# A hybrid RWKV-7 / gated-DeltaNet block: the gate pass's banks are emptied right behind two small steps on ScalarE, and three weight splits move back

## The reference, cut to what matters

```python
xn = rmsnorm(x, norm_mix_pre)
p = (xn @ w_in)                                   # 256 x (3 x 2048 + LoRA + 3 x 2048 + z + gates)
# RWKV-7 half, 32 heads x 64
p_rwkv = p_rwkv + (token_shift(p_rwkv) - p_rwkv) * rwkv_mix
kk = l2norm(k * rwkv_k_k);  k = k * (1 + (a - 1) * rwkv_k_a)
y = rwkv7_recurrence(r, decay, k, v, -kk, kk * a)  # then GroupNorm, bonus, gate
# gated DeltaNet half, 16 heads x 128, chunks of 64 frames
qkv = silu(causal_depthwise_conv(p_qkv, gdn_conv_w))
q, k = l2norm(q) * 128 ** -0.5, l2norm(k)
o = gated_delta_rule_chunked(q, k, v, g, beta)
y_b = rmsnorm(o, gdn_norm_w) * silu(z)
mixed = sigmoid(gate_a) * y_a + sigmoid(gate_b) * y_b
x = x + rmsnorm(mixed @ w_out, norm_mix_post)
x = x + rmsnorm((silu(rmsnorm(x) @ w_gate) * (rmsnorm(x) @ w_up)) @ w_down)
```

## Time and profile before

| | |
|---|---|
| time, median of 3 | 2225.74 us (2225.69 to 2225.81) |
| the profiled execution | 2224.51 us, of which the span of the core's instructions is 2222.8 |
| mean granted TensorE clock | 0.98 |
| busy: PE, PEld, DVE, ACT, POOL | 94%, 81%, 64%, 49%, 7% |
| one unit of the loop, q24 to q24 | 77.95 to 79.59 us |

### The profile page before, as it was taken

One profiled execution on the slowest core, in us unless ns is written; L12 is line 12 of the kernel. 1 busy time (PEld: TensorE's weight loads), 2 busy tenths in 40 slices (PEclk: granted clock), 3 DMA queues, 4 the chain that ended last, 5 costly groups with the idle time before them and its releaser, 6 DMA issues. The chain is left out here.

```text
span 2222.8 us, 49299 instructions
## 1 busy us (share of the span) xinstructions
PE 2092.7 (94%) x20515; PEld 1808.3 (81%) x20515; DVE 1420.4 (64%) x2816; ACT 1089.3 (49%) x2051; POOL 160.3 (7%) x277
## 2 busy tenths in 40 slices
PE   5999999999999999999999999499999999999995
PEld 5888888888888888888888889478888888778884
DVE  5568777777877877787787775544544445444444
ACT  4545554655555565555555545434444444344443
POOL 3001011011011101101110110000000000000000
PEclk9999999999999999999999999799999999999998
DMA  7654444545444455444544435175555555545542
GB/s 203 172 142 125 119 122 122 145 120 129 128 126 124 118 131 135 122 124 119 144 119 120 116 111 162 43 246 187 188 189 189 189 189 189 178 161 186 185 186 86
DMA packets 386637, 327.27 MB, mean 147 GB/s; under 512 B 11697, under 2 KB 334225, under 8 KB 379793
## 3 DMA queue, kind: packets, MB, share of 16 engines
q1 hardware_dynamic: 372384, 318.53, 48.8%
q10 hardware_dynamic: 14064, 6.04, 1.1%
HBM read 322.44 MB, written 2.10 MB: 146 GB/s over the span
## 5 line engine op out<-in xcount | busy, mean ns | idle before, releaser
L247 PE MATMUL ps<-hi_all,xh 128*128 128x384 f32 (+1 forms) x1568 | 564.0, 360 | 31.7 <-ACT pu L273 28.9
L1736 DVE TENSOR_TENSOR lo_all<-stage,hi_all 128x1024 fp32r<-128x1024 f32 x264 | 323.3, 1225 | 385.3 <-ACT hi_all L1731 385.3
L249 PE MATMUL ps<-hi_all,xl 128*128 128x384 f32 (+1 forms) x1568 | 531.8, 339 | 0.0
L248 PE MATMUL ps<-lo_all,xh 128*128 128x384 f32 (+1 forms) x1568 | 530.7, 338 | 0.0
L1731 ACT ACTIVATE hi_all<-stage 128x1024 fp32r<-128x1024 f32 x264 | 279.9, 1061 | 433.7 <-PE ps L1749 427.3
L242 DVE TENSOR_TENSOR lo_all<-stage,hi_all 128x768 fp32r<-128x768 f32 (+1 forms) x400 | 377.9, 965 | 120.5 <-ACT hi_all L237 119.7
L237 ACT ACTIVATE hi_all<-stage 128x768 fp32r<-128x768 f32 (+1 forms) x400 | 327.7, 833 | 217.6 <-PE ps L249 210.9
L247 PEld LDWEIGHTS ps<-hi_all,xh 128*128 128x128 f32 x1568 | 295.8, 189 | 67.6 <-ACT pu L273 36.2
L248 PEld LDWEIGHTS ps<-lo_all,xh 128*128 128x128 f32 x1568 | 296.8, 189 | 0.9
L249 PEld LDWEIGHTS ps<-hi_all,xl 128*128 128x128 f32 x1568 | 296.4, 189 | 0.9
L1745 PE MATMUL ps<-hi_all,xh 128*128 128x512 f32 x704 | 276.8, 393 | 10.0 <-DVE lo_all L1736 10.0
(11 more groups left out here) (277 smaller groups left out, 2655.3 us busy)
## 6 DMA issues: line engine op xcount, KB each, us to landing
stage<-in_w_in SPq DMA_DIRECT2D x288, 512.0 KB, 5.7
stage<-in_ffn_w_gate SPq DMA_DIRECT2D x44, 1024.0 KB, 5.2
stage<-in_ffn_w_up SPq DMA_DIRECT2D x44, 1024.0 KB, 5.2
stage<-in_ffn_w_down SPq DMA_DIRECT2D x22, 2048.0 KB, 7.6
stage<-in_w_out SPq DMA_DIRECT2D x16, 344.0 KB, 4.3
stage<-in_w_out SPq DMA_DIRECT2D x8, 516.0 KB, 4.6
stage<-in_w_in SPq DMA_DIRECT2D x8, 448.0 KB, 6.9
stage<-in_w_out SPq DMA_DIRECT2D x8, 336.0 KB, 4.6
```

The costliest lines, as they stand in the source:

```text
L247: nc.tensor.matmul(o, xh[:, kc, xs], high, start=kc == 0, stop=False)
L248: nc.tensor.matmul(o, xh[:, kc, xs], low, start=False, stop=False)
L249: return nc.tensor.matmul(o, xl[:, kc, xs], high, start=False, stop=kc == KC - 1)
L1736: nc.vector.tensor_tensor(wlo[s.par], src, whi[s.par].bitcast(F32), ALU.subtract).then_inc(s.lo, 1)
```

## The change

`chunk_act` gets a callback that it runs right behind its copy of r. The ACT list of a unit now has the squares, `r2`, `take_out(2)`, the two `stw` scalings (wa2, wb2), step (2, 2) with the two copies of u2, and then both weight splits (quanta 26 and 27) at once; one of them stood ahead of `r2` before, the other behind `take_out`. In unit 0 there is no r2, and `take_out` stands right behind the squares. On DVE quantum 26's split moves from ahead of the norm sums to behind the root and step (3, 2), beside quantum 27's.

```diff
-            def chunk_act(act, u, lag, k, c):
+            def chunk_act(act, u, lag, k, c, between=None):
...
                 if k == 1:
                     wait(act, EB, f"r{c}", u, lag)
                     fn(f"r{c}", rhs[:], ps[:, 4, 0:CH])
+                    if between:
+                        between()
                     if c in (1, 2):
                         for h, hp in enumerate(HALF):
                             fn(f"w{'ab'[h]}{c}", stw[hp, :], sv[hp, c, h, :], scale=wlast[hp, c:c + 1])
...
                 fn("sqq", sq[:, 1:3, :], qkv[:, 0:2, :], ACT.Square)
-                fill(1)
-                chunk(1, 2)
-                take_out(act, u, 2)
-                fill(1)
+                if prev:
+                    chunk_act(act, u, 1, 1, 2, lambda: take_out(act, u, 2))
+                else:
+                    take_out(act, u, 2)
                 chunk(2, 2)
+                fill(2)
                 chunk(3, 2)
...
                 chunk(1, 2)
-                fill(2)
+                fill(1)
                 after(E, "norms")
...
                 chunk(3, 2)
-                fill(1)
+                fill(2)
                 after(A, "ege")
```

## The result

The changed kernel takes 2200.86 us (median of 4 runs, 2199.09 to 2202.84) against 2225.74 before: ratio 0.9888, 95% interval 0.9874 to 0.9902. It is 24.9 us faster, where 20.1 were forecast, and lies 0.14 us under the low end of the range, 2201.0. The profiled execution took 2199.09 us with a span of 2197.4, so in the profiles 25.4 us are to be accounted for.

The account below looks back on a forecast made before the run. PE bounds the kernel, waiting for the PSUM banks' copies. 12.5 + 0.7 (unit 0) + 1.1 (unit 15) + 6.3 (clock) - 0.5 (`rhg`) = 20.1 us off, giving 2205.6 us; range 2201.0 to 2212.0.

Parts of the forecast that it names:

- The wait at quantum 24: PE's 0.89 us wait per unit behind the gate pass, for the PSUM banks' copies, goes whole; banks 0.63 us ahead.
- 14 x 0.89 = 12.5: Gain from removing PE's wait at quantum 24 in the fourteen units 1 to 14: 12.5 us.
- Unmoved, the root is in time; DVE's move is a margin: DVE's root ends at 657.58 even unmoved, PE wants it at 657.82; moving DVE's split gains nothing itself in units 1-14.
- g3: 0 to 0.1, taken 0.5 us in all: PE's new wait for DVE's `rhg` at step (2, 3): 0 to 0.1 us per unit, 0.5 us taken off.
- The clock: four falls, 6.3 us: PE's clock falls at quantum 24 in units 3, 6, 9 and 12 all go: 4 x 1.57 = 6.3 us.
- rival B: The wait goes but clock falls stay, at quantum 24 or behind the transposes: 2211.9, or 2207 to 2212; chance 0.24.
- Unit 15: 1.1 us, its clock left to the range: Two waits at quantum 24, 0.59 + 0.54, go; 2.5 us from the low clock behind is left to the range.
- Behind the loop: Clock falls at the joints after the loop: one more or less there is 1.6 us either way.
- 0.1 for unit 0: Unit 0's wait at quantum 24 goes, a gain of 0.70 us at most, 0.7 in the sum.
- D: Norm sums or u2 wait for something the banks' wait hid; the time stays about 2225; chance 0.03.
- E: Clock falls more often, at quantum 24 and behind the transposes; twenty falls give 2236.5, 10.8 us slower; chance 0.03.
- C: DVE holds PE: `rhg` late by half a microsecond or more in each of 14 units, 2212 to 2218; chance 0.08.

Follow-up runs that it names:

- Run 3: Changed kernel, with ACT making split 26 between its copy of r and the banks' copies: 2209.8 us, ratio 0.9924 to the kernel before.
- run 7: The changed kernel again, unaltered: 2200.67 us, ratio 0.9884 to the kernel before.
- Run 1: Changed kernel, with DVE's splits 25 and 26 both ahead of the norm sums again (ACT's part alone): 2241.57 us, ratio 1.0073 to the kernel before.
- Run 9: Kernel before in its own order, each pass's first quantum waiting for the first bank's copy alone, the second's three matmuls later: 2201.1 us, ratio 0.9891.
- Run 10: Changed kernel, with split 26 ahead of the banks' copies and one more ScalarE square into scratch ahead of r2 (units 0 to 14): 2213.02 us, ratio 0.9941.
- run 8: Changed kernel, each pass's first quantum waiting for the first bank's copy alone, the second's three matmuls later: 2189.27 us, ratio 0.9838 to the kernel before.
- run 4: Changed kernel, with PE's norm sums computed three times over, same values: 2275.06 us, ratio 1.0221 to the kernel before.
- run 5: Changed kernel, with PE's norm sums computed twice, same values: 2237.04 us, ratio 1.0053 to the kernel before.
- run 6: Changed kernel, with PE's norm sums and the four decay matmuls computed twice, same values: 2240.33 us, ratio 1.0066 to the kernel before.
- run 2: Kernel before, with DVE's part of the change alone: 2227.25 us, ratio 1.0006 to the kernel before.

## Why the prediction was right about the mechanism and short in size

- *The wait at quantum 24 goes.* Right, in its place and its cover: 0.64 us from squares to banks (0.64 forecast). The banks are done at 643.73 and PE's last matmul ahead of quantum 24 ends at 643.98 + 0.38 = 644.36: 0.63 us of cover (0.63 forecast). Run 3 takes the cover away and the wait is back, at 0.16.
- *14 x 0.89 = 12.5.* Too small. A plain unit went from 77.95 to 76.9 us, 1.05, so 14.7 us. The stretch from r2 to quantum 24 got 0.96 shorter, not 0.89: the idle time in the row counts from the end of the last matmul, 644.36 in the changed kernel, but the next one, when it need not wait, starts before that end, at 644.29. These 0.07 us come off with the wait. The remaining 0.1 comes later in the unit, among the small matmuls of the triangular inverses; why is open, and run 7's execution of the same kernel doesn't have it: its plain unit of 77.02 us is 0.94 shorter than before. So 13.4 of the 14.7 us are the wait, and the rest belongs to the one execution that was profiled.
- *Unmoved, the root is in time; DVE's move is a margin.* Wrong. I took the old end of the root, 657.58, and missed that ACT's reordering itself makes split 26's high part late. Run 1 shows the price, 2.1 us per unit and a kernel slower than before. This is a fault in the mechanism. It did no harm to the number, since the change has both parts.
- *g3: 0 to 0.1, taken 0.5 us in all.* The slack was used up as worked out: step (2, 3) moved up 0.03 us less than quantum 25 did, and the time is regained by quantum 27. 0.5 us too much was taken off. In unit 15, which the text didn't look at for this, DVE has a `w_out` split, the rest of the mixed rows (L396) and another split ahead of g3, and PE stands idle ahead of the step, 0.59 us:

```profile
1267.90 0.36 DVE L1314 SCALAR_TENSOR_TENSOR rhg<-ps,nege,vb 64x128 f32<-64x128 f32 x1
1268.36 0.33 PE L859 MATMUL ps<-rhs,xit 64*64 64x64 f32 x4 [0.59 <-issue]
```

The row names no releaser, but `rhg` is done at 1268.26, 0.10 us ahead of PE, and ACT's copy of r long before.
- *The clock: four falls, 6.3 us.* Right. 1019.77 - 999.81 = 20.0 us over thirteen units, of which 13 x 1.05 = 13.7 are the waits and 6.3 the falls. Runs 9 and 10 show that they go with half the wait as well. The strict reading of the Trainium skill's page ("TensorE: Matmul & The Clock Gate", What's actually happening), by which falls would stay as long as the norm sums are there (rival B), is not borne out: they are still there, and six profiles (after and runs 3, 7, 8, 9 and 10) have no fall in units 1 to 14. What the fall needs, length of the stretch or idle time in it, stays open (runs 4 to 6).
- *Unit 15: 1.1 us, its clock left to the range.* Here the sum was furthest off for its size. The stretch shortened by 3.0: 1.6 up to its first `w_out` quantum (the clock was low in part of that already), and 1.4 net behind it. There the 5.0 us at 0.50 clock of the earlier trace rows are at 1.00 now, which gives 2.1 up to step (1, 3); 0.7 of it is lost again ahead of step (2, 3), with the wait for g3. The text put 2.5 us on this clock and left it out of the number.
- *Behind the loop*, 0.6 us, within the 1.6 that was allowed.

So the step of the prediction that failed is the size of two terms of its sum. 14 x 0.89 = 12.5 measured 14.7, 2.2 us short, and unit 15's 1.1 measured 3.0, 1.9 short, mostly because the fall behind it was left out of the number. With 0.5 for g3, 0.1 for unit 0 and 0.6 behind the loop these are the 5.3 us between the 20.1 forecast and the 25.4 found in the profiles (by the medians it is 4.7). The range's low end had unit 15 and one fall in it, but not that the wait itself could be worth more than its idle time. Rivals B, D and E did not happen. C's mechanism, DVE holding PE, exists, at 0.03 us in the units of the loop and at 0.59 in unit 15, once in place of fourteen times; E needed more falls, and there are fewer.

## What to carry to other kernels

When an engine's list is reordered, follow each item that moves back to whoever waits for it: here the gain of one list was a loss until the other list moved too. Price a removed wait from instruction to instruction on the engine that waits, not by the idle time in its row. Before moving work around a wait for a pair of buffers, see whether the first user needs both: waiting bank by bank gave in the old order what this change gave, and 11.4 us more on top of it.

## What the runs showed of the hardware that was not expected

- TensorE's clock fell behind stretches of small matmuls in which the profile counts PE as busy for most of the time. In the kernel before, 3.37 us from r2 to quantum 24 with 0.89 idle were followed by a fall in 4 of the 14 units (5 in run 2), each costing 1.5 to 1.6 us. The 2.9 to 3.0 us of runs 9 and 10, with about 0.5 idle, were not in any of those units, and in run 6's nine units of 3.38 us with none idle the clock had not fallen when quantum 24 started. Whether the length or the idle time decides is open. The Trainium skill ("TensorE: Matmul & The Clock Gate", What's actually happening) lets the ratio follow how busy PE has been recently; the trace agrees in that every fall of units 1 to 14 has idle time ahead of it, in one case of run 5 only 0.30 us.
- Long rows of small matmuls run PE dry: with 192 norm sums of one or two columns in a row, PE stood still for 2.09 us within them in unit 7; with 128, for 0.2 to 3.7 us, within them or just behind, in some units and not in others; with 64, as in the changed kernel, not at all in units 1 to 14. The reason isn't shown; only that PE waited for no semaphore.
- With the falls in the loop gone, the kernel's four runs spread over 3.75 us, where those of the kernel before lay 0.12 apart. In the three later batches the kernel before spread over 2.9, 2.4 and 1.9 us itself, so this is not a property of the change.
